# Dense feed-forward stages of a one-core kernel: gate and value products with the weights stationary instead of the tokens, inner values left turned

## What is computed

```python
def rms_norm(x, g):
    y = xf * lax.rsqrt(jnp.mean(xf * xf, axis=-1, keepdims=True) + NORM_EPS)
    return y * g
...
def swiglu(u, w1, w2):
    gate, up = jnp.split(u @ w1, 2, axis=-1)
    return (jax.nn.silu(gate) * up) @ w2
...
h = h + 0.5 * rms_norm(swiglu(rms_norm(h, g[0]), ffn_w1[i, 0], ffn_w2[i, 0]), g[1])
```

## Time and profile before

| | |
|---|---|
| Median of 3 runs | 3358.28 us (3352.33 to 3360.78) |
| Profiled execution | 3354.18 us, span of its instructions 3352.3 us |
| Mean granted TensorE clock | 0.975 of 2.4 GHz |
| TensorE busy | 3183.7 us (95%) |
| VectorE busy | 2259.7 us (67%) |
| ScalarE busy | 1870.2 us (56%) |

### The profile page before, as it was taken

How to read it: one execution, slowest core, us unless ns; L and a number is a source line. 1 busy time by engine, 2 the same in 40 slices (tenths; PEclk the granted TensorE clock), 3 DMA queues, 4 the chain that set the end, 5 groups by cost and what they waited for, 6 DMA issues and landing times.

```text
span 3352.3 us, 41787 instructions
## 1 busy us (share of the span) xinstructions
PE 3183.7 (95%) x15980; PEld 2665.0 (79%) x15980; DVE 2259.7 (67%) x2676; ACT 1870.2 (56%) x2461; POOL 14.4 (0%) x26
## 2 busy tenths in 40 slices
PE   6999989999999989999899999997999999999998
PEld 5878578788887877888688788886888888788886
DVE  4549855555445565656554647555998898898997
ACT  4441354544555445646444447463777777777775
POOL 0000000000000000000000000000000000000000
PEclk9999999999999989999899999997999999999999
DMA  8444265555436444534454344434999999999994
GB/s 271 163 157 151 75 201 170 183 191 172 132 101 208 138 176 151 186 132 152 166 195 176 139 151 151 142 122 162 350 365 353 333 366 354 333 366 354 355 355 185
DMA packets 381165, 719.10 MB, mean 215 GB/s; under 512 B 14025, under 2 KB 153743, under 8 KB 380847
## 3 DMA queue, kind: packets, MB, share of 16 engines
q1 hardware_dynamic: 376384, 707.71, 59.6%
q0 software_dynamic: 2368, 8.52, 0.7%
q10 hardware_dynamic: 2223, 0.31, 0.1%
HBM read 715.44 MB, written 1.05 MB: 214 GB/s over the span
## 4 chain that ended last, share of the span: by engine, by line
PE 89%; DVE 5%; ACT 4%; issue 1%; ACTq 0%; DMA 0%; DVEq 0%; SPq 0%
PE duo L1011 13%; PE duo L1012 13%; PE duo L1013 13%; PE acc L1011 8%; PE acc L1013 8%; PE acc L1012 8%; PE aux L1011 2%; PE aux L1013 2%; PE aux L1012 2%; PE duo L387 1%; PE duo L542 1%; PE duo L543 1%; PE duo L544 1%; PE aux L542 1%; PE aux L543 1%; PE aux L544 1%
## 5 line engine op out<-in xcount | busy, mean ns | idle before, releaser
L1583 DVE TENSOR_TENSOR weights_split<-w,weights_split 128x1024 fp32r<-128x1024 f32 x672 | 790.6, 1221 | 107.9 <-ACT weights_split L1562 106.8
L1562 ACT ACTIVATE weights_split<-w 128x1024 fp32r<-128x1024 f32 x672 | 677.6, 1057 | 247.6 <-PE duo L1013 168.1
L1011 PE MATMUL duo<-weights_split,u_high 128*128 128x512 f32 x1776 | 699.7, 394 | 10.7 <-issue 5.8
L1013 PE MATMUL duo<-weights_split,u_low 128*128 128x512 f32 x1776 | 694.0, 391 | 1.4 <-issue 1.4
L1012 PE MATMUL duo<-weights_split,u_high 128*128 128x512 f32 x1776 | 693.8, 391 | 0.0
L416 DVE TENSOR_TENSOR w_low<-w,w_high 128x1024 fp32r<-128x1024 f32 x304 | 368.4, 1223 | 329.6 <-ACT w_high L407 328.7
L1128 DVE TENSOR_TENSOR weights_split<-w,weights_split 128x1024 fp32r<-128x1024 f32 x320 | 377.7, 1222 | 283.8 <-ACT weights_split L1116 283.6
L407 ACT ACTIVATE w_high<-w 128x1024 fp32r<-128x1024 f32 x304 | 318.1, 1057 | 348.8 <-PE acc L1013 96.3
L1116 ACT ACTIVATE weights_split<-w 128x1024 fp32r<-128x1024 f32 x320 | 322.3, 1058 | 256.6 <-PE duo L1013 155.6
L1011 PEld LDWEIGHTS duo<-weights_split,u_high 128*128 128x128 f32 x1776 | 335.6, 189 | 81.2 <-issue 13.3
L1013 PEld LDWEIGHTS duo<-weights_split,u_low 128*128 128x128 f32 x1776 | 334.9, 189 | 70.7
(11 more groups left out here) (409 smaller groups left out, 5041.8 us busy)
## 6 DMA issues: line engine op xcount, KB each, us to landing
w<-in_ffn_w_dram SPq DMA_DIRECT2D x132, 1024.0 KB, 7.6
w<-in_moe_w_gate_dram SPq DMA_DIRECT2D x112, 1024.0 KB, 7.2
w<-in_moe_w_up_dram SPq DMA_DIRECT2D x112, 1024.0 KB, 7.2
w<-in_moe_w_down_dram SPq DMA_DIRECT2D x112, 1024.0 KB, 8.0
w<-in_w_in_dram SPq DMA_DIRECT2D x92, 1024.0 KB, 7.2
w<-in_hyb_w_in_dram SPq DMA_DIRECT2D x18, 1024.0 KB, 7.4
w<-in_ffn_w_gate_dram SPq DMA_DIRECT2D x11, 1024.0 KB, 7.6
w<-in_ffn_w_up_dram SPq DMA_DIRECT2D x11, 1024.0 KB, 10.0
```

Source lines behind the costliest of these rows:

```text
L1011: pe.matmul(bank_out, x_hi, w_hi, start=first, stop=False, skip_group_check=True)
L1013: return pe.matmul(bank_out, x_lo, w_hi, start=False, stop=last, skip_group_check=True)
L1562: act.activation(units[:, place, 0, cut], src[:, cut], ACT.Copy).then_inc(sem("moe_high"), 1)
L1583: m = dve.tensor_tensor(units[:, place, 1, cut], src[:, cut], units[:, place, 0, cut], ALU.subtract)
```

## The change

In the dense stages the gate and value products are made by `turned_products`. Bank 4 + c now belongs to half `c` of the block's 256 inner columns and holds the gate for 256 tokens and the value for 256 tokens. Each half has two groups (gate and value) x 4 chunks x 2 units x 3 matmuls of 256 moving columns: 96 matmuls in an `up`. `hid` comes out with the inner columns on the partitions, `turn` is gone, and the high and low parts are made from `hid` itself in SBUF.

A token's factor is no longer one value per partition, since tokens now lie along the free axis. In scaled stages it is made into a row: VectorE spreads it into `scale_wide`, TensorE transposes that once per stage (`turn_scale`, inside the first `up`, into bank 6), ScalarE copies it to `scale_row`, and VectorE multiplies the gate by it (`gate_scaled`) before SiLU. The value product takes no factor; it comes in at the stage's output, as `out_rms` inside the sum of squares and `out_scale` (with the 0.5) in the first multiplication of the post-norm. A few semaphores at the kernel's start are merged.

```diff
         def act_postnorm_sums(key, t):
 
+            dense = key not in ("mixA", "mixB")
+            if dense:
+                act.wait_ge(sem("token_scale"), at("token_scale", (key, "out")))
...
                 m = act.activation(junk[:, t, half * 512:(half + 1) * 512], acc[:, i, :], ACT.Square,
-                                   scale=D ** -0.5, accum_out=ssq[:, 4 + i:5 + i])
+                                   scale=out_rms[:, t:t + 1] if dense else D ** -0.5, accum_out=ssq[:, 4 + i:5 + i])
...
-        silu = view(4096, NT, 256)
-        hid = view(4608, NT, 256)
-        hidT = view(5120, 2, T)
+        silu, hid = view(4096, 2, T), view(4608, 2, T)
+        scale_row, scale_wide = u[:, 0, :], split(u[:, 1, :], NT)
...
                         elif x == 0:
 
-                            pe.wait_ge(sem("hidden_ready"), hid0 + 2 * j + t + 1 + 2 * body * i)
-                        cut = slice(t * P, (t + 1) * P)
-                        for k in range(4):
-                            m = products(bank(4 + t), uh[:, 4 * x + k, cut], ul[:, 4 * x + k, cut],
-                                         whi[:, k, :], wlo[:, k, :], first=(x == 0 and k == 0),
-                                         last=(x == 1 and k == 3))
+                            pe.wait_ge(sem("hidden_ready"), hid0 + 2 * j + c + 1 + 2 * body * i)
+                        if x == 1 and c == 1 and j < 0 and scaled:
+                            turn_scale()
+                        for y in range(2):
+                            cut = slice(y * 256 + c * P, y * 256 + (c + 1) * P)
+                            for k in range(4):
+                                m = turned_products(bank(4 + c)[:, y * T:(y + 1) * T], whi[:, k, cut], wlo[:, k, cut],
+                                                    uh[:, 4 * x + k, :], ul[:, 4 * x + k, :],
+                                                    first=(x == 0 and y == 0 and k == 0),
+                                                    last=(x == 1 and k == 3))
...
-            def turn(i, j):
-                if j < 0:
-                    claim(6)
-                pe.wait_ge(sem("hidden_ready"), hid0 + 2 * (j + 2) + 2 * body * i)
-                for c in range(2):
-                    for t in range(NT):
-                        m = pe.transpose(bank(6)[:, c * T + t * P:c * T + (t + 1) * P],
-                                         hid[:, t, c * P:(c + 1) * P], cst("ident"))
-                m.then_inc(bank_full(6), 1)
+            def turn_scale():
+
+                claim(6)
+                pe.wait_ge(sem("token_scale"), at("token_scale", (key, "wide")))
+                for t in range(NT):
+                    m = pe.transpose(bank(6)[:, t * P:(t + 1) * P], scale_wide[:, t, :], cst("ident"))
+                m.then_inc(bank_full(6), fill(6, (key, "scale")))
...
                 if j >= 0:
-                    down(i, j - 1, 0, first=(j == 0))
-                turn(i, j)
-                if j >= 0:
-                    down(i, j - 1, 1, first=(j == 0))
+                    for t in range(NT):
+                        down(i, j - 1, t, first=(j == 0))
...
                 if j < 0 and scaled:
-                    act.wait_ge(sem("token_scale"), at("token_scale", key))
-                for t in range(NT):
-                    act.wait_ge(bank_full(4 + t), full0[t] + 2 + j + body * i)
-                    act.activation(silu[:, t, :], bank(4 + t)[:, 0:256], ACT.Silu,
-                                   scale=token_scale[:, t:t + 1] if scaled else 1.0)\
+                    act.wait_ge(bank_full(6), filled_at(6, (key, "scale")))
+                    act.activation(scale_row[:, :], bank(6)[:, 0:T], ACT.Copy)\
+                       .then_inc(sem("scale_row"), mark("scale_row", key))
+                    was_read(6, (key, "scale"), "scale_row")
+                for c in range(2):
+                    if scaled:
+                        act.wait_ge(sem("gate_scaled"), gate0 + 2 * (1 + j) + c + 1 + 2 * body * i)
+                    else:
+                        act.wait_ge(bank_full(4 + c), full0[c] + 2 + j + body * i)
+                    act.activation(silu[:, c, :], silu[:, c, :] if scaled else bank(4 + c)[:, 0:T], ACT.Silu)\
                        .then_inc(sem("silu_ready"), 1)
...
+                if j < 0 and scaled:
+                    dve.wait_ge(sem("scale_row"), at("scale_row", key))
+                if scaled:
+                    for c in range(2):
+                        dve.wait_ge(bank_full(4 + c), full0[c] + 2 + j + body * i)
+                        dve.tensor_tensor(silu[:, c, :], bank(4 + c)[:, 0:T], scale_row[:, :], ALU.mult)\
+                           .then_inc(sem("gate_scaled"), 1)
...
+                for c in range(2):
+                    dve.wait_ge(sem("silu_ready"), silu0 + 2 * (1 + j) + c + 1 + 2 * body * i)
+                    dve.tensor_tensor(hid[:, c, :], silu[:, c, :], bank(4 + c)[:, T:2 * T], ALU.mult)\
+                       .then_inc(sem("hidden_ready"), 1)
```

74 lines of the change are left out of this document (42 added, 32 removed).

## The result

| | before | changed kernel |
|---|---|---|
| Median of 4 runs each | 3357.95 us (3352.33 to 3360.78) | 3391.18 us (3388.67 to 3394.38) |
| Ratio, 95% interval | | 1.0102 (1.0084 to 1.0119) |
| Profiled execution | 3354.18 us | 3394.38 us |
| Mean granted clock | 0.975 | 0.968 |

The change costs 33.2 us by the medians, 40.2 us between the two profiled executions (the profiled one of the changed kernel is the slowest of its four). The forecast was 26 us won. 3391.18 us is outside the range of 3322 to 3353 us.

The account below looks back on a forecast made before the run. Dense stages were taken as bound by TensorE, busy for all of the steady windows. Turns -23.5, starts -2.8, the rest 0 gave -26.3 us: median 3358.3 to 3332.0 us, range 3322 to 3353.

Parts of the forecast that it names:

- price of 256 columns: Dense `up`: 96 matmuls of 256 columns at 113.3 ns take 10.88 us, no difference from 48 at 226.7 ns.
- 50 turns removed: Dense steps: four transposes per step go, 0.47 us for each of 50 turns, 23.5 us won.
- two multiplications, chain to `hid`: Steady dense step: VectorE's extra multiplications and a chain of about 1.5 us, hidden under `down`, cost nothing.
- pause after the first `up`: Stage starts: 0.3 us won in each of four scaled stages, 1.6 us in the unscaled one, 2.8 us together.
- So I price the new matmul by proportion: Dense `up`: half of 226.7 ns, 113.3 ns per 256-column matmul, because the mixers show no fixed part.
- a fixed part of 13.4 ns at 512 columns: Dense matmuls: 226.7 ns less 213.3 ns for 512 columns at 2.4 GHz, taken as a possible fixed cost per matmul.
- the upper bound: Dense `up`: 13.4 ns fixed cost added to 106.7 ns gives 120 ns per 256-column matmul.
- six rows at 120 ns: Mixed block: six matmuls with 256 moving columns took 0.72 us, 120 ns each.
- the exact halving in the mixers: Mixers: 256 columns at 116.7 ns cost exactly half of 512 at 233.3 ns, read as no fixed part.
- Rival 2: Dense `up`: fixed cost per weight load, 120 ns a matmul, period 16.96 us, 8.9 us lost, 3367.2 us; chance 9%.
- the Trainium skill's formula: Dense `up`: N / 2.4 + 2.5 ns gives 109.2 ns; 6.9 us longer over 55, total gain 19.4 us.
- the table load and SiLU 0: First `up` of scaled stages: table loaded by 43.5, SiLU 0 done by 44.0, next `up` at 44.5, 0.3 us won.

Follow-up runs that it names:

- e1: Kernel before, tokens still stationary, every 512-column gate and value matmul cut into two of 256: 3403.44 us, ratio 1.0136.
- e11: Kernel before without its turns, high and low parts copied from `hid` as it lies, so results are wrong: 3325.95 us, ratio 0.9912.
- e4: Kernel before, with the first `up` of each dense stage waiting for both token halves before its first matmul: 3372.78 us, ratio 1.0044.
- e13: Changed kernel plus 12 matmuls of 8 columns on constants before each dense stage's first gate and value products: 3391.15 us, ratio 1.0097.
- e14: Changed kernel plus 6 matmuls of 8 columns on constants before each dense stage's first gate and value products: 3387.83 us, ratio 1.0091.
- e16: Changed kernel plus 240 already met semaphore waits behind TensorE's first transposes of the program: 3386.60 us, ratio 1.0086.
- e8: Kernel before, with the four quarters of the activations turned and split in the order 0, 2, 1, 3: 3360.46 us, ratio 1.0009.
- e3: Kernel before, with the SBUF tiles after the constants moved by 32 bytes: 3361.81 us, ratio 1.0012.
- e7: Changed kernel, with activation quarters in the order 0, 2, 1, 3 and gate and value regions written by turns: 3382.79 us, ratio 1.0079.

## Why the prediction was wrong, step by step

Its steps against what was measured, in us over the kernel:

| step | forecast | measured | from |
|---|---|---|---|
| price of 256 columns | 0 | +35 | 55 x 96 x 6.67 ns; e1 |
| 50 turns removed | -23.5 | -23.5 | period of e11 |
| two multiplications, chain to `hid` | 0 | 0 | steady windows |
| pause after the first `up` | -2.8 | -3.1 | gaps below |
| first product waits for both halves | not seen | +11 | times to the first product; e4 |
| low clock in the first `up` | not seen | +5 | slow matmuls |
| place of the instructions | not seen | some +9 (4 to 10 by the other kernels) | e13, e14, e16 |

The sum is +33, of 33.2 by the medians and 40.2 between the profiled executions. The 7 us that are missing to the latter lie outside the dense stages, and no run explains them; e8, which changes nothing there, differs there from the kernel before by 2.2 us, e3 by 6.9 (of which its dearer mixer matmuls, 2400 x 1.1 ns, are 2.6), and the profiled execution before was 4 us under its median. That the sum meets the medians so closely is in part luck, since the last row is known to some 3 us only.

**The step that failed** is the sentence "So I price the new matmul by proportion". The two marks for it were in the rows: a fixed part of 13.4 ns at 512 columns, and 213 ns per 256 columns at half clock with nothing beside it, which give 120 ns. Both were worked out and used only as the upper bound, six rows at 120 ns were set aside, and the exact halving in the mixers (116.7 to 233.3) was believed to hold where its own base, 233.3, did not. In place of 113.3 ns the runs showed 120, in the changed kernel and in e1: +35 us in place of 0. The halving itself held only at those addresses (117.8 and 233.3 in e3). A stage with another price at 512 columns was no witness for this one at 256. Rival 2, given 9%, had the fixed cost as mechanism, the price and the period (16.96 for 16.98). Its sum of +8.9 us lacked only the starts and the instructions' place. One sum beside the forecast is off, the one by the Trainium skill's formula: 55 x 0.12 are 6.6 us, not 6.9, and the gain by it would be 19.7 us.

**The second failure** is a step that was not there. Part by part, the change was followed through the steady step, the pause and the end, but not through the first matmul of the stage: what must be ready for it. The wait for both halves is visible in the code. From the transposes to the first product the five stages now take 9.41, 6.36, 6.08, 6.72 and 8.71 us, before 6.91, 4.28, 3.81, 4.23 and 7.23: 10.8 us by this, 11 in the table. And more of the first `up`s falls in stretches of lower clock: 98 matmuls at 213 ns for 120 are 9.1 us, before 21 at 427 for 227 are 4.2. That the wait is the reason is likely, since e4 alone goes from 21 to 40 such matmuls of 512 columns, but in single stages it does not follow the length of the wait (e7 above).

**Right** were the turns (e11), and the cover of the longer chain. Between the last gate matmul and `hid` lie, in the changed kernel's timelines of VectorE and ScalarE:

```profile
59.51 0.42 DVE L1218 TENSOR_TENSOR arena<-duo,u 128x256 f32<-128x256 f32 x1 [1.91 <-PE duo L545]
...
60.42 0.42 DVE L1224 TENSOR_TENSOR arena<-arena,duo 128x256 f32<-128x256 f32 x1 [0.15 <-ACT arena L1183]
```

The chain ends at 60.84, 1.5 us behind the start of `down` at 59.31, as estimated, and `down` lasts 5.47. The pause after the first `up` has the size forecast. TensorE's rows, then VectorE's:

```profile
46.51 0.28 PE L545 MATMUL duo<-u_high,weights_split 128*128 128x256 f32 x1
47.72 0.36 PE L543 MATMUL duo<-u_high,weights_split 128*128 128x256 f32 x1 [0.93 <-DVE arena L1224]
```
```profile
46.83 0.42 DVE L1218 TENSOR_TENSOR arena<-duo,u 128x256 f32<-128x256 f32 x1 [2.02 <-PE duo L545]
47.17 0.41 DVE L1224 TENSOR_TENSOR arena<-arena,duo 128x256 f32<-128x256 f32 x1
```

1.21 us from start to start, less the pitch of 0.12, is 1.09 lost, 1.72 before: 0.63 less, with 0.25 for the two scale transposes 0.38 won, 0.3 forecast. The unscaled stage has no pause any more, 1.6 won, as forecast. In the scaled stages, though, the agreement is luck. The forecast had the table load and SiLU 0 set the time. They were done by 46.08 (L1183, 45.66 + 0.42); the product of half 0 (47.17) came only behind the scaling of gate 1 (46.83), which is ahead of it in VectorE's order and waits for the last matmul of the `up`.

**Open** stays why the mixers' matmuls cost 116.7 and 233.3 ns where the dense ones cost 120 and 226.7: addresses by 32 bytes and the order of groups do not explain it. Open too is what in the instructions' place brings the second idle time, what places the stretches of lower clock, and whether the fixed part is the matmul's or its weight load's.

## What to carry to other kernels

A matmul's price is columns over clock plus a fixed part; cutting the moving operand in half pays the fixed part twice, so take it from the longest run of the same loop, where it shows as the excess over one column per cycle, and not from a proportion seen in another stage. When the stationary and the moving operand change places, ask of the first product of every stage which data it now needs: here 23.5 us of removed transposes were worth less than 35 us of fixed parts and 16 us of starts. And a change in the number of instructions ahead of a loop can move its time by some 7 us with nothing in it changed, so a difference of that size in an untouched stretch wants a padded kernel beside it before it is explained.

## What the hardware showed that I had not expected

- The price by moving columns of float32r matmuls with a weight load each, at granted clock 1.00: 64 columns 112 ns, 128 111, 256 120, 384 174, 448 202, 512 226.7. At 0.50, 256 columns take 213 and 512 take 427 ns, without the fixed part.
- The low clock in a first `up` did not follow the length of the idle time just ahead of it: 15 matmuls at 213 ns behind 0.89 us (e7, stage 2), none behind 1.73 us (e7, stage 3), 25 behind 2.21 us (changed kernel, stage 3), and none behind 1.99 us in e16's first stage, although TensorE had stood idle for 12 us shortly before.
- Idle times of 1.9 and 2.2 us, put down to issue, in a loop 2600 us behind the place where 240 waits were added, are there without them and gone with them.
- A met wait on a semaphore takes TensorE's queue 50 ns (e16: 240 in 12.1 us).
- In the expert part a 16 KB packet of the instruction queue starts with each idle time of some 3 us that is put down to issue, in all traces.
